# State space layer: u times d moves into the tap matrices, gelu reads PSUM, two direct terms move ahead

## The chip, the cores and the metric

The kernel runs on one core of one Trainium2 chip. The metric is the device time of one execution in microseconds; lower is better. Three runs of the kernel before took 2245.55, 2247.62 and 2248.52 us, median 2247.62. A run of its own was taken with the hardware profiler, and all rows below are from that one.

Engine names: PE (TensorE) multiplies matrices, PEld is its weight load, DVE is VectorE, ACT is ScalarE, POOL is GpSimd, SP is the queue that issues the weight transfers. Each engine runs its own program in order and waits on semaphores for the others.

## The reference, cut to what matters

The program is one block of a first model (state space layer beside a sliding window attention, then a feed-forward layer) and two blocks of a second model. Only the state space layer is touched. `u` is 512 tokens by 512 features, in 32 groups of 16 features with 64 complex states each:

```python
def s5_mixer(u, lam_re, lam_im, log_dt, b_re, b_im, c_re, c_im, d, w_glu, b_glu):
    uf = u.astype(jnp.float32).reshape(bsz, L, SSM_GROUPS, SSM_GROUP)
    ...                                  # discretised a and bbar
    bu_re = jnp.einsum('blgh,gph->blgp', uf, bbar_re)
    bu_im = jnp.einsum('blgh,gph->blgp', uf, bbar_im)
    _, _, xr, xi = lax.associative_scan(_s5_combine, (a_re, a_im, bu_re, bu_im), axis=1)
    y = (jnp.einsum('blgp,ghp->blgh', xr, c_re) - jnp.einsum('blgp,ghp->blgh', xi, c_im)
         + d.astype(jnp.float32) * uf)
    y = jax.nn.gelu(y.reshape(bsz, L, SSM_WIDTH))
    z = y @ w_glu + b_glu
    return z[..., :SSM_WIDTH] * jax.nn.sigmoid(z[..., SSM_WIDTH:])
```

The attention of the same block (8 query heads of 64, window 128) takes q, k and v from the same projection and needs nothing of the state space layer.

## The kernel before, in words

All is kept with features on the 128 partitions and the 512 tokens along the row, so the 512 features of the state space layer are four tiles, i = 0 to 3, of 128x512. PSUM is one tensor `ps` of eight banks of 128x512.

**Time steps in chunks of 4** (`STEP` = 4, 128 chunks). Inside a chunk the output is a convolution: `direct_weights` multiplies out the tap matrices for lags tau = 0 to 3 (128 matmuls of 128x32 into bank 6), ACT copies them to `k_tau`, and `ssm_direct(i)` applies them to `u`: four matmuls of 512, 384, 256 and 128 columns. Between chunks there is a scan: `ssm_in(bt)` takes `u` to the chunk inputs of two tiles (64 matmuls), DVE turns them by cos and sin (`modulate`), scans them along the chunks and turns them back (`demodulate`), and `ssm_out(i)` adds what this gives to the same bank as `ssm_direct(i)` (32 matmuls of 127 columns). Two batches of two tiles: `bt` = 0 holds tiles 0 and 1, `bt` = 1 tiles 2 and 3.

**From there to the GLU.** `ssm_direct` and `ssm_out` of tile i go to bank 6 for even i and to bank 7 (`SUM`) for odd i, so tile 2 can start only when tile 0 has been read (`pre_gelu`). `ssm_chunk(c)` on DVE reads the bank, adds `u` times `d` and writes a row in time order to `tmp`. ACT takes the gelu of it (L1360), then writes the rounded part `x_hi` (`part_hi`), and DVE the rest `x_lo` (`part_lo`). Big products are made of three such parts (`w_lo*x_hi + w_hi*x_lo + w_hi*x_hi`).

**Beside it, the attention.** `turn_tokens1` on PE makes the swapped k and q for the rotary embedding (banks 3 and `Q1_BANKS`) and turns v (bank 0); `rotate1` on DVE finishes each in three passes. Then come 16 steps s. In each PE does `turn1(s)` (turns the weights p), `scores1(s+2)`, `glu_part(s)` (some of the 32 units of the GLU product) and `values1(s-1)`; DVE copies the turned weights (L2136), takes `maximum1(s+2)` and `scale1(s-1)`; ACT takes the exponentials. PE's first scores wait for `kr1_ready`, two of `qr1_ready` and `vt1_ready`; `turn1(0)` waits for the exponentials of step 0; `values1(s)` waits until `scale1(s-1)` has read bank 6 (`o1_ready`).

**What sets the order.** Nothing is scheduled by a planner: each engine's program is written by hand in the order shown. The DVE order around the change is `modulate(0)`, `demodulate(0)`, `modulate(1)`, `demodulate(1)`, `ssm_chunk` 0 and 1, k and q tile 0 rotated, `part_lo` 0 and 1, `ssm_chunk(2)`, q tile 1, `part_lo(2)`, `ssm_chunk(3)`, the two first maxima, `part_lo(3)`, q tile 2, then the 16 steps. The weights come by SP in slabs of up to 1 MB into two slots; the load of slab n is issued when DVE has split slab n-2 (`wlo_ready`).

Of the kernel before, what the change touches and what calls it, by code (L numbers as in the profile page):

```python
# [15 lines left out]
P = 128  # L16
T = 512
# [78 lines left out]
def build(nc, w, x_in, gains_in, lam_in, sink_in, bc_in, c_in, pos_in, iota_in, const_in, freq_in, mask_in, rope2_in,  # L96
# [123 lines left out]
    part_im = at("part_im", where["tmp"] + 4 * KB, [N_PAIR // 2, CHUNKS])  # L220
    pos = at("pos", where["tmp"], [T], i32)
# [26 lines left out]
    def by_phase(bank):  # L248

        return bank.rearrange("p (c l) -> p l c", l=STEP)  # L250

# [104 lines left out]
    v_ready = sem("v_ready")  # L356
    yssm_done = sem("yssm_done")
# [51 lines left out]
    Q1_BANKS = (4, 5, 1, 2)  # L409
    GLU_PER_STEP = [2] * 8 + [3] * 5 + [1, 0, 0]  # L410
# [62 lines left out]
    with nc.Block() as block:  # L473
# [77 lines left out]
        def _(pe):  # L551
# [189 lines left out]
            def direct_weights():  # L741

                for i in range(4):
                    for tau in range(STEP):
                        for ab, cc in ((ab_re, c_re), (ab_neg, c_im)):
                            for q in range(4):
                                at_ = GW * (STEP * i + tau)
                                last = pe.matmul(ps[GW * q:GW * q + GW, 6, at_:at_ + GW], ab[:, tau, 4 * i + q, :],
                                                 cc[:, 4 * i + q, :], start=cc is c_re, stop=cc is c_im)
                last.then_inc(kt_done, 1)  # L750
# [41 lines left out]
            def ssm_direct(i):  # L792
                if i >= 2:
                    pe.wait_ge(pre_gelu, i - 1)
                for tau in range(STEP):
                    pe.matmul(ps[:, (6, SUM)[i % 2], P * tau:T], k_tau[:, i, tau, :],
                              u[:, i, 0:STEP - tau, :].rearrange("p l c -> p (l c)"), start=tau == 0, stop=False,
                              skip_group_check=True)

            def ssm_out(i):  # L800
                for l in range(STEP):
                    for ca, v in ((ca_re, v_re), (ca_im, v_im)):
                        for q in range(4):
                            last = pe.matmul(ps[GW * q:GW * q + GW, (6, SUM)[i % 2], P * l + 1:P * l + P],
                                             ca[:, l, 4 * i + q, :], v[:, 4 * i + q, 0:CHUNKS - 1], start=False,
                                             stop=l == STEP - 1 and ca is ca_im, skip_group_check=True)
                last.then_inc(yssm_done, 1)

            def turn_tokens1():

                pe.wait_ge(bu_free, BATCHES)
                pe.matmul(ps[:, 3, :], swap1, k1[:, :], start=True, stop=True).then_inc(kr1_swap, 1)
                for c in range(4):
                    pe.matmul(ps[:, Q1_BANKS[c], :], swap1, q1[:, c, :], start=True, stop=True).then_inc(qr1_swap, 1)
                for b in range(TB):
                    last = pe.transpose(ps[:, 0, b * P:(b + 1) * P], v1[:, b * P:(b + 1) * P], ident)
                last.then_inc(vt1_done, 1)

# [8 lines left out]
            ssm_in(1)  # L827
            pe.wait_ge(ca_ready, 1)
            for bt in range(BATCHES):
                pe.wait_ge(v_ready, bt + 1)  # L830
                for ii in range(2):
                    if bt:
                        ssm_direct(2 * bt + ii)
                    ssm_out(2 * bt + ii)
                if bt == 0:
                    turn_tokens1()
# [70 lines left out]
            scores1(1)  # L907
            for s in range(16):
# [356 lines left out]
        def _(act):  # L1265
# [88 lines left out]
            act.wait_ge(vt1_done, 1)  # L1354
            act.activation(v1_tok[:, :, :].rearrange("p a c -> p (a c)"), ps[:, 0, :], ACT.Copy).then_inc(vt1_ready, 1)
            for i in range(4):
                act.wait_ge(pre_gelu, i + 1)
                if i >= 2:
                    act.wait_ge(xlo_ready, XB["w_glu"] + i - 1)
                act.activation(tmp[:, 2 + i % 2, :], tmp[:, i % 2, :], ACT.Gelu_apprx_tanh)  # L1360
                act.drain()
                part_hi("w_glu", i, tmp[:, 2 + i % 2, :])
# [353 lines left out]
        def _(dve):  # L1716
# [287 lines left out]
            take(9)  # L2004
            settle()

            def ssm_chunk(c):
                dve.wait_ge(yssm_done, c + 1)
                if c >= 2:
                    dve.wait_ge(xlo_ready, XB["w_glu"] + c - 1)  # L2010
                stt(by_phase(tmp[:, c % 2, :]), u[:, c, :, :], gain("d", c),
                    ps[:, (6, SUM)[c % 2], :].rearrange("p (l c) -> p l c", l=STEP), ALU.mult, ALU.add) \
                    .then_inc(pre_gelu, 1)
# [61 lines left out]
            ssm_chunk(0)  # L2075
            ssm_chunk(1)
# [3 lines left out]
            part_lo("w_glu", 0, tmp[:, 2, :])  # L2080
            part_lo("w_glu", 1, tmp[:, 3, :])
            ssm_chunk(2)
            rotate_q1(1)
            part_lo("w_glu", 2, tmp[:, 2, :])
            ssm_chunk(3)
# [43 lines left out]
            part_lo("w_glu", 3, tmp[:, 3, :])  # L2129
# [637 lines left out]
```

## Time and profile before

| | |
|---|---|
| three runs, median | 2245.55 to 2248.52 us, 2247.62 us |
| the profiled execution, its own time | 2243.69 us |
| its span, first to last instruction | 2241.9 us |
| PE busy | 2137.8 us, 95% |
| DVE busy | 1280.1 us, 57% |
| ACT busy | 886.7 us, 40% |
| chain that ended last, by engine | PE 81%, DVE 11%, DVE's sequencer 4%, ACT 2% |
| mean granted TensorE clock | 0.968 of full |

The profiled execution is 1.79 us longer than its span, and 3.93 us below the median of the three runs. The share of busy time is a mean over the whole program; the stage that is touched is a small piece of it, from about 92 to about 215 us after the start. A row of a timeline says when an instruction (or a merged run of like ones, with its count) started, how long it lasted, and in brackets how long its engine had been idle before it and who ended that. An fp32 matmul stands as two matmul instructions in the trace, so the counts there are twice those of the program.

### The profile page before, as it was taken

The numbers are of one execution on the slowest core, as the hardware profiler recorded it, in microseconds if no ns is written. First come the engines' busy times: TensorE is split into PE (matmuls) and PEld (weight loads), VectorE is DVE, ScalarE is ACT, GpSimd is POOL, SyncE is SP. The second block draws the span as 40 slices with busy tenths as digits, with TensorE's granted clock in tenths as the row PEclk, the third lists the DMA queues.
The fourth block names the chain that finished last, engine by engine and source line by source line (L and its number), as shares of the span: only waits on it lengthen the run. The fifth ranks groups of instructions, "written<-read, shape, count | busy, mean of one in ns | idle before, by whom it ended". The sixth has DMA issues, their size and how long they took to land.

```text
span 2241.9 us, 29415 instructions
## 1 busy us (share of the span) xinstructions
PE 2137.8 (95%) x11002; PEld 1741.6 (78%) x11002; DVE 1280.1 (57%) x2043; ACT 886.7 (40%) x1298; POOL 69.3 (3%) x63
## 2 busy tenths in 40 slices
PE   7969999999999999999988999999999998999997
PEld 5757778888877888888877788888777876888886
DVE  6987454434454666666676642344568886433444
ACT  4225232222227556566552431242345524322322
POOL 1000300000130000000000000000000000000000
PEclk8988999999999999999999899999999998999998
DMA  4102222232232212212221223222112221222221
GB/s 168 30 10 78 93 75 94 86 114 100 71 117 85 85 59 74 85 66 70 80 76 52 76 97 109 94 94 94 57 58 75 75 76 67 102 94 94 94 96 55
DMA packets 31518, 183.46 MB, mean 82 GB/s; under 512 B 5184, under 2 KB 5568, under 8 KB 12736
## 3 DMA queue, kind: packets, MB, share of 16 engines
q1 hardware_dynamic: 27504, 176.18, 23.1%
q10 hardware_dynamic: 3024, 6.00, 0.8%
q8 instruction: 55, 0.90, 0.2%
q0 software_dynamic: 896, 0.06, 0.0%
q14 instruction: 39, 0.32, 0.0%
HBM read 180.06 MB, written 2.10 MB: 81 GB/s over the span
## 4 chain that ended last, share of the span: by engine, by line
PE 81%; DVE 11%; DVEq 4%; ACT 2%; issue 1%; DMA 1%; ACTq 0%
PE ps L569 12%; PE ps L571 12%; PE ps L570 12%; PE ps L1058 6%; PE ps L1060 5%; PE ps L1059 5%; PE ps L1114 2%; PE ps L1115 2%; PE ps L1116 2%; PE ps L630 1%; PE ps L620 1%; PE ps L599 1%; PE ps L625 1%; PE ps L969 1%; DVE f_run L2608 1%
## 5 line engine op out<-in xcount | busy, mean ns | idle before, releaser
L1284 ACT ACTIVATE w_hi<-raw 128x2048 fp32r<-128x2048 f32 (+1 forms) x122 | 226.0, 1853 | 297.1 <-PE ps L571 220.2
L569 PE MATMUL ps<-x_hi,w_lo 128*128 128x512 f32 x816 | 317.6, 389 | 0.5 <-DVE y L2205 0.3
L571 PE MATMUL ps<-x_hi,w_hi 128*128 128x512 f32 x816 | 317.5, 389 | 0.0
L570 PE MATMUL ps<-x_lo,w_hi 128*128 128x512 f32 x816 | 317.4, 389 | 0.0
L1725 DVE TENSOR_TENSOR w_lo<-raw,w_hi 128x2048 fp32r<-128x2048 f32 (+3 forms) x116 | 259.3, 2235 | 93.1 <-ACT w_hi L1284 92.6
L1058 PE MATMUL ps<-x_hi,w_lo 128*128 128x512 f32 x544 | 218.8, 402 | 2.9 <-DVE w_lo L2375 2.4
L1060 PE MATMUL ps<-x_hi,w_hi 128*128 128x512 f32 x544 | 213.1, 392 | 0.0
L1059 PE MATMUL ps<-x_lo,w_hi 128*128 128x512 f32 x544 | 212.5, 391 | 0.0
L569 PEld LDWEIGHTS ps<-x_hi,w_lo 128*128 128x128 f32 x816 | 153.2, 188 | 32.9 <-issue 0.7
L570 PEld LDWEIGHTS ps<-x_lo,w_hi 128*128 128x128 f32 x816 | 153.2, 188 | 31.9
L571 PEld LDWEIGHTS ps<-x_hi,w_hi 128*128 128x128 f32 x816 | 153.2, 188 | 31.8
L571 PE MATMUL ps<-hid_hi,w_hi 128*128 128x512 f32 x378 | 147.1, 389 | 0.0
L569 PE MATMUL ps<-hid_hi,w_lo 128*128 128x512 f32 x378 | 147.0, 389 | 0.0
L570 PE MATMUL ps<-hid_lo,w_hi 128*128 128x512 f32 x378 | 147.0, 389 | 0.0
L2375 DVE TENSOR_TENSOR w_lo<-raw,w_hi 128x2048 fp32r<-128x2048 f32 x38 | 87.0, 2290 | 84.2 <-ACT w_hi L1497 76.6
L2411 DVE TENSOR_TENSOR tmp<-tmp 128x512 f32<-128x512 f32 x64 | 44.3, 692 | 145.6 <-ACT hid_hi L1577 145.5
L1058 PEld LDWEIGHTS ps<-x_hi,w_lo 128*128 128x128 f32 x544 | 102.7, 189 | 24.2 <-DVE w_lo L2375 2.8
L1060 PEld LDWEIGHTS ps<-x_hi,w_hi 128*128 128x128 f32 x544 | 102.5, 188 | 22.4
L1059 PEld LDWEIGHTS ps<-x_lo,w_hi 128*128 128x128 f32 x544 | 102.7, 189 | 19.6
L1539 ACT ACTIVATE swapped<-ps 32x512 f32<-32x512 f32 x192 | 113.2, 590 | 2.3
L1575 ACT ACTIVATE tmp<-ps 128x512 f32<-128x512 f32 x64 | 38.3, 599 | 178.4 <-PE ps L571 175.5
L1530 ACT ACTIVATE qkv<-ps 128x512 f32<-128x512 f32 x72 | 43.0, 598 | 132.0 <-PE ps L1060 131.9
(453 smaller groups left out, 3966.5 us busy)
## 6 DMA issues: line engine op xcount, KB each, us to landing
raw<-w_attn_in SPq DMA_DIRECT2D x32, 1024.0 KB, 5.0
raw<-w_gate_up SPq DMA_DIRECT2D x22, 1024.0 KB, 4.9
raw<-w_up_a SPq DMA_DIRECT2D x16, 1024.0 KB, 4.9
raw<-w_down_a SPq DMA_DIRECT2D x16, 1024.0 KB, 4.9
raw<-w_up_h SPq DMA_DIRECT2D x16, 1024.0 KB, 5.0
raw<-w_down_h SPq DMA_DIRECT2D x16, 1024.0 KB, 4.9
raw<-w_hgrn_in SPq DMA_DIRECT2D x8, 1024.0 KB, 4.9
raw<-w_down SPq DMA_DIRECT2D x8, 768.0 KB, 4.3
```

The costliest lines, as they stand in the source:

```text
L569: pe.matmul(o, w_lo[:, slot, a:a + P], hi[:, k, :], start=k == 0, stop=False)
L570: pe.matmul(o, w_hi[:, slot, a:a + P], lo[:, k, :], start=False, stop=False)
L571: last = pe.matmul(o, w_hi[:, slot, a:a + P], hi[:, k, :], start=False, stop=k == st.kc - 1)
L1058: pe.matmul(o, w_lo[:, slot, a:a + P], x_hi[:, k, :], start=k == 0, stop=False)
L1059: pe.matmul(o, w_hi[:, slot, a:a + P], x_lo[:, k, :], start=False, stop=False)
L1060: last = pe.matmul(o, w_hi[:, slot, a:a + P], x_hi[:, k, :], start=False, stop=k == DC - 1)
L1114: pe.matmul(o, w_lo[:, slot, a:a + P], hi[:, k, :], start=k == 0, stop=False, skip_group_check=True)
L1115: pe.matmul(o, w_hi[:, slot, a:a + P], lo[:, k, :], start=False, stop=False, skip_group_check=True)
L1284: act.activation(w_hi[:, slot, 0:width], raw[:, slot, 0:width], ACT.Copy).then_inc(whi_ready, 1)
L1539: last = act.activation(turned[to:to + 32], bank[at_:at_ + 32], ACT.Copy)
L1725: tt(w_lo[:, slot, 0:width], raw[:, slot, 0:width], w_hi[:, slot, 0:width].bitcast(f32), ALU.subtract) \
L2375: tt(w_lo[:, n0 % 2, :], raw[:, n0 % 2, :], w_hi[:, n0 % 2, :].bitcast(f32), ALU.subtract) \
```

## The change

The term `u*d` is put into the tap matrix of lag 0. DVE makes `d_diag`, the identity times `d` (four 128x128 operations, in the place of the tensor `root`), and `direct_weights` adds it with four matmuls of 128x32 for each of the four tiles. `ssm_chunk` is gone: ACT takes the gelu from the PSUM bank itself and writes it in time order over the tile of `u` that is no longer needed (`glu_in`); `pre_gelu` is now counted by ACT, and `part_hi` and `part_lo` read `glu_in`. A small gelu is issued on ACT ahead of the waits, which puts the table load there. The four tiles have a bank each (`Y_BANKS`), so `ssm_direct(2)` and `ssm_direct(3)` are issued before the first `ssm_out`. The turned v goes to bank 2, and the swaps of q tiles 2 and 3, which share banks with it and with y tile 2, are issued after the two first scores.

The diff, cut to its core:

```diff
@@ -218,6 +218,7 @@
+    d_diag = at("d_diag", where["root"], [4, P])
@@ -248,6 +249,10 @@
+    def glu_in(i):
...
+        return u[:, i, :, :].rearrange("p l c -> p (l c)")
@@ -354,6 +359,7 @@
+    diag_ready = sem("diag_ready")
@@ -407,6 +413,7 @@
+    Y_BANKS = (6, 7, 1, 0)
@@ -740,13 +747,18 @@
+                pe.wait_ge(diag_ready, 1)
...
+                        at_ = GW * (STEP * i + tau)
...
-                                at_ = GW * (STEP * i + tau)
...
-                                                 cc[:, 4 * i + q, :], start=cc is c_re, stop=cc is c_im)
+                                                 cc[:, 4 * i + q, :], start=cc is c_re, stop=cc is c_im and tau > 0)
+                        if tau == 0:
+                            for q in range(4):
+                                last = pe.matmul(ps[GW * q:GW * q + GW, 6, at_:at_ + GW], ident[:, GW * q:GW * q + GW],
+                                                 d_diag[:, i, GW * q:GW * q + GW], start=False, stop=True)
@@ -790,10 +802,8 @@
-                if i >= 2:
-                    pe.wait_ge(pre_gelu, i - 1)
...
-                    pe.matmul(ps[:, (6, SUM)[i % 2], P * tau:T], k_tau[:, i, tau, :],
+                    pe.matmul(ps[:, Y_BANKS[i], P * tau:T], k_tau[:, i, tau, :],
@@ -801,7 +811,7 @@
-                            last = pe.matmul(ps[GW * q:GW * q + GW, (6, SUM)[i % 2], P * l + 1:P * l + P],
+                            last = pe.matmul(ps[GW * q:GW * q + GW, Y_BANKS[i], P * l + 1:P * l + P],
@@ -810,11 +820,14 @@
-                for c in range(4):
-                    pe.matmul(ps[:, Q1_BANKS[c], :], swap1, q1[:, c, :], start=True, stop=True).then_inc(qr1_swap, 1)
+                for c in range(2):
+                    swap_q1(c)
...
-                    last = pe.transpose(ps[:, 0, b * P:(b + 1) * P], v1[:, b * P:(b + 1) * P], ident)
+                    last = pe.transpose(ps[:, 2, b * P:(b + 1) * P], v1[:, b * P:(b + 1) * P], ident)
...
+            def swap_q1(c):
+                pe.matmul(ps[:, Q1_BANKS[c], :], swap1, q1[:, c, :], start=True, stop=True).then_inc(qr1_swap, 1)
@@ -825,12 +838,13 @@
+            pe.wait_ge(tile_free["dve"], STAGES["w_in"].tiles)
+            ssm_direct(2)
+            ssm_direct(3)
...
-                    if bt:
-                        ssm_direct(2 * bt + ii)
@@ -905,6 +919,9 @@
+            pe.wait_ge(pre_gelu, 3)
+            swap_q1(2)
+            swap_q1(3)
@@ -1351,15 +1368,17 @@
-            act.wait_ge(vt1_done, 1)
-            act.activation(v1_tok[:, :, :].rearrange("p a c -> p (a c)"), ps[:, 0, :], ACT.Copy).then_inc(vt1_ready, 1)
+            act.activation(half_glu, gains[:, 0:4], ACT.Gelu_apprx_tanh)
...
-                act.wait_ge(pre_gelu, i + 1)
-                if i >= 2:
-                    act.wait_ge(xlo_ready, XB["w_glu"] + i - 1)
-                act.activation(tmp[:, 2 + i % 2, :], tmp[:, i % 2, :], ACT.Gelu_apprx_tanh)
+                if i == 2:
+                    act.wait_ge(vt1_done, 1)
+                    act.activation(v1_tok[:, :, :].rearrange("p a c -> p (a c)"), ps[:, 2, :], ACT.Copy).then_inc(vt1_ready, 1)
+                act.wait_ge(yssm_done, i + 1)
+                act.activation(glu_in(i).rearrange("p (c l) -> p l c", l=STEP),
+                               ps[:, Y_BANKS[i], :].rearrange("p (l c) -> p l c", l=STEP), ACT.Gelu_apprx_tanh) \
+                   .then_inc(pre_gelu, 1)
...
-                part_hi("w_glu", i, tmp[:, 2 + i % 2, :])
+                part_hi("w_glu", i, glu_in(i))
@@ -2002,15 +2021,11 @@
+            dve.wait_ge(consts_ready, 16)
+            for c in range(4):
+                last = ts(d_diag[:, c, :], ident, gain("d", c), None, ALU.mult)
+            last.then_inc(diag_ready, 1)
...
-            def ssm_chunk(c):
-                dve.wait_ge(yssm_done, c + 1)
-                if c >= 2:
-                    dve.wait_ge(xlo_ready, XB["w_glu"] + c - 1)
-                stt(by_phase(tmp[:, c % 2, :]), u[:, c, :, :], gain("d", c),
-                    ps[:, (6, SUM)[c % 2], :].rearrange("p (l c) -> p l c", l=STEP), ALU.mult, ALU.add) \
-                    .then_inc(pre_gelu, 1)
@@ -2072,17 +2087,12 @@
-            ssm_chunk(0)
-            ssm_chunk(1)
...
-            part_lo("w_glu", 0, tmp[:, 2, :])
-            part_lo("w_glu", 1, tmp[:, 3, :])
-            ssm_chunk(2)
...
-            part_lo("w_glu", 2, tmp[:, 2, :])
-            ssm_chunk(3)
+            for c in range(3):
+                part_lo("w_glu", c, glu_in(c))
@@ -2126,7 +2136,7 @@
-            part_lo("w_glu", 3, tmp[:, 3, :])
+            part_lo("w_glu", 3, glu_in(3))
```

The order on PE, in the middle of the state space layer, before (`ssm_out`'s end, the swaps and turns of k, q and v, the second batch's `ssm_direct` and the first rows of its `ssm_out`):

```order
L804 MATMUL ps<-v_im,ca_im 32x127 x4
L812 MATMUL ps<-k_79,consts 128x512 [waits bu_free]
L814 MATMUL ps<-q_60,consts 128x512 x4
L816 MATMUL ps<-consts,v_80 128x128 x4
L796 MATMUL ps<-u,k_tau 128x512 [waits pre_gelu,v_ready]
L796 MATMUL ps<-u,k_tau 128x384
L796 MATMUL ps<-u,k_tau 128x256
L796 MATMUL ps<-u,k_tau 128x128
L804 MATMUL ps<-v_re,ca_re 32x127 x4
```

And of the changed kernel at the same place:

```order
L814 MATMUL ps<-v_im,ca_im 32x127 x4
L822 MATMUL ps<-k_79,consts 128x512 [waits bu_free]
L830 MATMUL ps<-q_60,consts 128x512 x2
L826 MATMUL ps<-consts,v_80 128x128 x4
L814 MATMUL ps<-v_re,ca_re 32x127 [waits v_ready]
L814 MATMUL ps<-v_re,ca_re 32x127 x3
L814 MATMUL ps<-v_im,ca_im 32x127 x4
```

Between the turned v and `ssm_out` of tile 2 the `ssm_direct` rows and the wait on `pre_gelu` are gone; two of the four q swaps are elsewhere. At the end of that stage, before (from the last `ssm_out` to the first turned weights):

```order
L804 MATMUL ps<-v_im,ca_im 32x127 x4
L850 MATMUL ps<-k_79,q_60 128x128 [waits kr1_ready,qr1_ready,vt1_ready,mask_ready]
L850 MATMUL ps<-k_79,q_60 128x128
L850 MATMUL ps<-k_79,q_60 128x256 x2
L863 MATMUL ps<-consts,p_83 128x128 [waits pre_gelu,p1_ready]
```

And of the changed kernel:

```order
L814 MATMUL ps<-v_im,ca_im 32x127 x4
L864 MATMUL ps<-k_79,q_60 128x128 [waits kr1_ready,qr1_ready,vt1_ready,mask_ready]
L864 MATMUL ps<-k_79,q_60 128x128
L864 MATMUL ps<-k_79,q_60 128x256 x2
L830 MATMUL ps<-q_60,consts 128x512 [waits pre_gelu]
L830 MATMUL ps<-q_60,consts 128x512
L877 MATMUL ps<-consts,p_83 128x128 [waits pre_gelu,p1_ready]
```

The two other q swaps now stand between the first scores and `turn1(0)`. On DVE, from the last pass of `demodulate(1)` to the first maximum, before:

```order
L2055 SCALAR_TENSOR_TENSOR v_im<-v_im,part_im 128x1024
L2011 SCALAR_TENSOR_TENSOR tmp<-u,gains,ps 128x4x128 [waits yssm_done] x2
L2065 TENSOR_TENSOR rot_82<-ps,rope_s 128x512 [waits kr1_swap]
L2066 TENSOR_TENSOR k_79<-k_79,rope_c 128x512
L2068 TENSOR_TENSOR k_79<-k_79,rot_82 128x512
L2065 TENSOR_TENSOR rot_82<-ps,rope_s 128x512 [waits qr1_swap]
L2066 TENSOR_TENSOR q_60<-q_60,rope_c 128x512
L2068 TENSOR_TENSOR q_60<-q_60,rot_82 128x512
L1748 TENSOR_TENSOR x_lo<-tmp,x_hi 128x512 [waits xhi_ready] x2
L2011 SCALAR_TENSOR_TENSOR tmp<-u,gains,ps 128x4x128 [waits xlo_ready,yssm_done]
```

And of the changed kernel:

```order
L2070 SCALAR_TENSOR_TENSOR v_im<-v_im,part_im 128x1024
L2080 TENSOR_TENSOR rot_82<-ps,rope_s 128x512 [waits kr1_swap]
L2081 TENSOR_TENSOR k_79<-k_79,rope_c 128x512
L2083 TENSOR_TENSOR k_79<-k_79,rot_82 128x512
L2080 TENSOR_TENSOR rot_82<-ps,rope_s 128x512 [waits qr1_swap]
L2081 TENSOR_TENSOR q_60<-q_60,rope_c 128x512
L2083 TENSOR_TENSOR q_60<-q_60,rot_82 128x512
L2080 TENSOR_TENSOR rot_82<-ps,rope_s 128x512 [waits qr1_swap]
L2081 TENSOR_TENSOR q_60<-q_60,rope_c 128x512
L2083 TENSOR_TENSOR q_60<-q_60,rot_82 128x512
L1767 TENSOR_TENSOR x_lo<-u,x_hi 128x512 [waits xhi_ready] x3
```

All four `ssm_chunk` rows (L2011) are gone from DVE, and the three first `part_lo` stand together behind the rotations.

## Rows read from the trace of the kernel before

**Rows 1.** Waits of PE from 90 to 215 us: total, times, longest.

```profile
PE ps L796 <- DVE tmp L2011: 10.6, 1, 10.6
PE ps L863 <- ACT stat L1390: 3.5, 1, 3.5
PE ps L804 <- DVEq L2056: 3.0, 1, 3.0
PE ps L796 <- ACT k_tau L1349: 2.5, 1, 2.5
PE ps L748 <- issue: 1.6, 1, 1.6
```

**Rows 2.** Waits of DVE in the same stretch.

```profile
DVE o_tok L2123 <- PE ps L902: 7.3, 10, 1.4
...
DVE tmp L2011 <- PE ps L804: 0.9, 2, 0.6
```

**Rows 3.** Timeline of DVE: start, duration, instruction, count, idle before and who ended it.

```profile
95.89 1.23 DVE L2029 TENSOR_TENSOR v_re<-ps,cos_c 128x1024 f32<-128x1024 f32 x1 [2.27 <-PE ps L788]
...
115.53 1.23 DVE L2029 TENSOR_TENSOR v_re<-ps,cos_c 128x1024 f32<-128x1024 f32 x1 [0.19 <-issue]
...
135.10 2.07 DVE L2011 SCALAR_TENSOR_TENSOR tmp<-u,gains,ps 128x512 f32<-128x512 f32 x2
137.02 0.67 DVE L2065 TENSOR_TENSOR rot<-ps,rope_s 128x512 f32<-128x512 f32 x1
...
140.94 1.29 DVE L1748 TENSOR_TENSOR x_lo<-tmp,x_hi 128x512 fp32r<-128x512 f32 x2
...
147.76 0.34 DVE L2105 CUSTOM_DVE_ANT_0 ps<-ps,masks 128x128 f32<-128x128 f32 x1
...
152.85 0.42 DVE L2136 COPY p_t<-ps 128x256 f32<-128x256 f32 x1
154.40 0.43 DVE L2105 CUSTOM_DVE_ANT_0 ps<-ps,masks 128x256 f32<-128x256 f32 x1 [1.13 <-PE ps L850]
...
158.79 0.43 DVE L2105 CUSTOM_DVE_ANT_0 ps<-ps,masks 128x256 f32<-128x256 f32 x1 [0.37 <-PE ps L850]
...
160.79 0.47 DVE L2123 TENSOR_SCALAR o_tok<-ps,stat 128x64 f32<-128x64 f32 x2 [0.27 <-PE ps L902]
```

**Rows 4.** Timeline of ACT.

```profile
126.43 1.28 ACT L1360 ACT_TABLE_LOAD   x1
136.25 0.63 ACT L1360 ACTIVATE tmp<-tmp 128x512 f32<-128x512 f32 x1 [8.54 <-DVE tmp L2011]
...
149.42 1.28 ACT L1388 ACT_TABLE_LOAD   x1
150.72 0.37 ACT L1388 ACTIVATE p<-ps,stat 128x128 f32<-128x128 f32 x1
```

**Rows 5.** Timeline of PE.

```profile
108.65 3.85 PE L788 MATMUL ps<-u,lw 32*128 32x128 f32 x128
...
121.75 3.60 PE L814 MATMUL ps<-q,consts 128*128 128x512 f32 x8
...
136.36 4.25 PE L796 MATMUL ps<-u,k_tau 128*128 128x512 f32 x8 [10.58 <-DVE tmp L2011]
...
142.42 2.42 PE L796 MATMUL ps<-u,k_tau 128*128 128x512 f32 x8
...
146.64 1.57 PE L850 MATMUL ps<-k,q 64*128 64x128 f32 x8
151.67 0.69 PE L863 MATMUL ps<-consts,p 128*128 128x128 f32 x2 [3.45 <-ACT stat L1390]
...
163.27 1.00 PE L902 MATMUL ps<-v_tok,p_t 128*128 128x64 f32 x8
```

**Rows 6.** Stretches: length, busy PE, PEld, DVE, ACT, POOL, PE clock, DMA share, GB/s.

```profile
151.60:154.00 2.40, 2.33 (x6) 1.45 (x6) 1.59 (x3) 1.96 (x7) 0.00 (x0) 0.50 0.00 0
157.00:160.50 3.50, 3.50 (x19) 2.65 (x18) 2.84 (x12) 0.25 (x1) 0.00 (x0) 0.97 0.00 0
```

## The prediction

> **What bounds the kernel now.** I read the page first, and it says little here: PE is busy 95% of the span, but as a mean over the whole program. The stage that is touched lies between 92 and 215 us, and there the waits of PE come first [rows 1]. These five are all that PE waits for in that stretch. The longest, 10.6 us, is before `ssm_direct(2)`: PE waits for DVE's `ssm_chunk(0)`. The next, 3.5 us, is before `turn1(0)`: PE waits for ACT's first exponentials. After 151.67 us PE waits for nothing until 215. So the stage has two halves: up to about 152 us DVE's program is the path, with no idle time from 115.53 on but the short waits for PE; after that PE is. The timeline of DVE shows the first half [rows 3]: `demodulate(1)` has just ended when two `ssm_chunk` start at 135.10, then come rotations, `part_lo`, two more `ssm_chunk`, and the first maximum at 147.76. The timelines of ACT and PE show what hangs on that: the first exponential at 150.72 [rows 4] and `turn1(0)` at 151.67 after 3.45 us of idle time [rows 5]. PE pays twice: in the stretch after that idle time it is granted 0.50 of its clock (1.2 GHz), and it is back at 0.97 only in the stretch from 157.0 [rows 6].
>
> **Edits that I cost at nothing.** *d_diag on DVE*: four operations of 128x128. Nearest are 0.34 (first maximum, 128x128) and 0.67 (128x512) [rows 3], so 1.4 to 2.7 us; I take 1.4, by size. They stand where DVE waited 2.27 us for `ssm_in(0)` [rows 3]; at the upper bound all would be 0.4 us later. *16 more matmuls in direct_weights*: `ssm_in` has 64 matmuls in 3.85 us [rows 5], 0.06 each, so at most 1.0 us, and not below 0. They push `ssm_in(1)`, whose end was 112.50; DVE asks for it at 115.53 [rows 3]. Cover 3.0 us. *ssm_direct(2) and (3) early*: 2.42 us each at full clock [rows 5], so PE goes on from about 113 to 118, and where it waited 3.0 us [rows 1] the first `ssm_out` is some 2 us later. That result goes to ACT now, and nobody needs tiles 0 and 1 before about 141. Then come the k swap, two q swaps (four took 3.60, so 0.9 each [rows 5]) and the turned v. Before, all this ended 10.58 us ahead of 136.36; that idle time is the cover, and PE still waits in it for DVE. *The table load ahead*: it changes nothing, for the load was early already: it ran at 126.43 while its gelu had to wait until 136.25 [rows 4].
>
> **DVE's path, step by step.** From 135.10, where the first `ssm_chunk` stood:
> - three rotations (k, q tiles 0 and 1): two took 140.94 - 137.02 = 3.92, so 1.96 each, 5.9: 141.0.
> - three `part_lo` at 1.29 for two, about 0.6 each: 142.8. All need ACT's `x_hi`; for tile 2 see below.
> - the first maximum at 142.8 and not 147.76: 5.0 us earlier. That is what four `ssm_chunk` cost (two in 2.07, so some 4.1) and the 0.9 that they waited for PE [rows 2].
> - from there to the copy of step 0, 152.85 - 147.76 = 5.1: 147.9.
> - the next maximum came 1.55 later, 1.13 of it waiting for PE. PE will have done those scores, so 148.3.
> - to the maximum after that 158.79 - 154.40 = 4.4, less 0.37 idle: 152.3.
> - to the scaling L2123 2.0, less 0.27 idle, and 0.47 for itself: 154.5. This lets `values1(1)` go.
>
> **PE and ACT beside it.** PE starts `ssm_out(2)` at 135.2. One tile takes 146.64 - 142.42 - 2.42 = 1.8 at full clock. After idle time of this length `ssm_direct(2)` took 4.25 against 2.42 for its twin, so at the lower clock. Two tiles take 3.6 at the higher and 7.2 at the lower; starting low and rising as late as in that row (136.36 + 4.25, so 4.2 us in, with 2.1 us of the work done), 140.9. Gelu of tile 2 is done by 140, of tile 3 by 141.5 (0.63 each), its `x_hi` by 142.2, the exponential's table (1.28) by 143.8 at the latest. The first scores start when q tile 1 is rotated, 141.0, against 146.64. The two q swaps behind them add 1.8, so PE is ready for `turn1(0)` at about 144.4. The first exponential needs the first maximum and its small operations, 1.2 us: 144.1. `turn1(0)` followed 0.95 later: 145.0, not 151.67. From `turn1(0)` to `values1(1)` PE took 163.27 - 151.67 = 11.6 us. Of these, 5.3 (up to 157.0) ran at half clock; PE will have idled less than 1 us this time and not 3.45, so I count them at full clock, 2.7: 8.9 us in all, so 153.9. DVE's 154.5 is later, and the `values1(1)` of before at 163.27 becomes 154.6: **8.7 us** earlier.
>
> **The sum.** From 163.27 on PE waited for nothing up to 215 [rows 1], and DVE waited 7.3 us for PE's values in ten places [rows 2], so DVE catches up and the 8.7 us stay. Every transfer is asked for when DVE has split a slab, and moves with it. The profiled execution took 2243.69, so 2243.69 - 8.7 = 2235.0; the median of the three runs is 3.93 above it, so **2239 us** is the forecast. Of the 8.7, 5.0 are DVE's work and waits gone, 1.8 its waits for PE in the first steps (1.13 + 0.37 + 0.27), and the other 1.9 that PE came to `values1(1)` that much after DVE had let it go, since it had been slow.
>
> **Two rules weighed.** The rows of the tables first: the exponential ran right at the end of its table load: 149.42 + 1.28, then 150.72 [rows 4]. The Trainium skill, page "ScalarE: Activation LUTs", section "What ACT_TABLE_LOAD costs", counts a drain of 1380 ns on top, 2.66 us in all. By the page the first exponential would come at about 145.1, and the sum would be 8.5; the trace bears that out in no row. Second: `ssm_chunk`, which wrote its row in steps of four elements, took 1.04 each where an ordinary pass took 0.67 [rows 3]. The Trainium skill, page "SBUF — State Buffer", its note on "cachelines", says that an access that goes to a new 16-byte line pays a penalty; the gelu now writes in just such steps. If it grows by the same 0.4 us, tile 3's comes at 141.9 and the table at 144.2: the sum stays.
>
> **The rivals.**
> - *TensorE comes cold to the steps again.* For: it idles some 10 us before 135.2, as before, and the clock may rise later than I take it. If `ssm_out` runs wholly at the lower clock, it ends at 142.4, the scores and swaps at twice their time (3.1 + 3.6) at about 149, and `values1(1)` at 149 + 8.9 = 158: 5.3 us gained. If it rises in time and falls again for `turn1(0)`, 145.0 + 11.6 = 156.6 leaves 6.7; both at once about 2.6. Middle 5: 2242.6. Against: in the trace it had risen by the end of the 4.25 us row.
> - *DVE's pace is all there is.* The steps follow DVE, and only its 5.0 us arrive: 2242.6. Against: its 7.3 us of waiting in the loop.
> - *Taken back.* Short matmuls in an unbroken row ran out of instructions once: 1.6 us within `direct_weights`, for which the profile shows no cause but issue [rows 1]. Now 16 more stand there and `ssm_out(2)`, `(3)` and the scores have no break. Two or more such stops on the path, with something late after the loop, leave under 4.5 us: about 2245.
> - *Slower: TensorE stays at the lower clock through the steps.* PE would now meet DVE in each step with short waits where before it was full. The stretch from 151.67 to 157.0 shows the price: 2.7 us lost in 5.3. If all of the 60 us of steps ran so, 30 us would be lost: 2239 + 30 = 2269. It takes over the gain from 17 us of steps at the lower clock. Against: the waits I find are under 1 us, and the steps of before held 0.97 once they had begun to fill [rows 6].
>
> **Chances.** Forecast 0.70 (its own range 2236 to 2241.5, three runs differing by 3 us); cold start 0.13; DVE's pace 0.08; taken back 0.05; slower 0.04. Two parts in a thousand, 4.5 us, are about what a measurement of this kernel can tell from no change. Faster by more: all of the forecast, two thirds of the next two, 0.84. Within it 0.12. Slower 0.04. Range 2235.5 to 2244: below, a warmer loop than I count; above, the mixed forms of the first three rivals.
>
> **What will show it.** No wait of PE for DVE's `tmp`; PE's idle time before `ssm_out(2)` about 10 us, ending near 135.2; the first maximum near 142.8; the first exponential near 144.1; PE idle under 1 us before `turn1(0)`, with the full clock there; `values1(1)` near 154.6 with a short wait for L2123's successor; from there the same steps as before. I am wrong if the clock from 141 to 150 is low, if gelu from PSUM takes well over 1 us, or if the distance at 163 us is 8.7 and is less at 215.

## The result, and the profile after

| | before | after |
|---|---|---|
| median of 4 runs each | 2246.85 us | 2233.03 us (2230.09 to 2234.72) |
| ratio, 95% interval | | 0.9944 (0.9928 to 0.9961) |
| the profiled execution, its span | 2243.69, 2241.9 us | 2233.89, 2232.1 us |
| mean granted TensorE clock | 0.968 | 0.972 |

The change gains 13.8 us where 8.7 were forecast; 2233.03 lies 2.5 us below the range. The direction was right, the size was not. The fourth run of the kernel before brought its median down by 0.8 us, from 2247.62 to 2246.85; that part of the distance to 2239 is not the change's.

PE's waits from 90 to 215 us of the changed kernel (line waited for, us in total, times, longest), against [rows 1]:

```profile
PE ps L814 <- DVEq L2071: 8.3, 1, 8.3
PE ps L756 <- issue: 4.0, 2, 2.5
PE ps L806 <- ACT k_tau L1366: 2.6, 1, 2.6
PE ps L877 <- ACT stat L1409: 0.9, 1, 0.9
```

The wait for `tmp` (10.6) is gone, as is the one ahead of the first `ssm_out` (3.0): the direct terms of tiles 2 and 3 are done there now. What is left is the one ahead of `ssm_out(2)`, and before `turn1(0)` (L877) 0.9 stands where 3.5 stood. Within `direct_weights` (L756) PE now stood still twice, 4.0 us and not 1.6, with no cause but issue.

DVE's timeline (start, us, instruction, idle time before it and who ended it), against [rows 3]:

```profile
97.54 1.22 DVE L2044 TENSOR_TENSOR v_re<-ps,cos_c 128x1024 f32<-128x1024 f32 x1 [1.48 <-PE ps L800]
...
117.95 1.22 DVE L2044 TENSOR_TENSOR v_re<-ps,cos_c 128x1024 f32<-128x1024 f32 x1 [0.97 <-PE ps L800]
...
137.51 0.69 DVE L2080 TENSOR_TENSOR rot<-ps,rope_s 128x512 f32<-128x512 f32 x1
...
145.22 0.29 DVE L2115 CUSTOM_DVE_ANT_0 ps<-ps,masks 128x128 f32<-128x128 f32 x1
...
156.19 0.48 DVE L2133 TENSOR_SCALAR o_tok<-ps,stat 128x64 f32<-128x64 f32 x2
```

The four `ssm_chunk` are gone. But `modulate(1)` now waits 0.97 us for `ssm_in(1)`, so it comes 20.41 us after `modulate(0)` and not 19.64 [rows 3]. From it the first maximum is 27.27 us away, where it was 32.23.

ACT's timeline, against [rows 4]:

```profile
106.91 1.28 ACT L1371 ACT_TABLE_LOAD   x1
...
124.26 1.18 ACT L1377 ACTIVATE u<-ps 128x512 f32<-128x512 f32 x1 [15.85 <-PE ps L814]
...
143.77 1.12 ACT L1377 ACTIVATE u<-ps 128x512 f32<-128x512 f32 x1 [0.78 <-PE ps L814]
...
145.75 1.28 ACT L1407 ACT_TABLE_LOAD   x1
147.04 0.37 ACT L1407 ACTIVATE p<-ps,stat 128x128 f32<-128x128 f32 x1
```

The gelu's table is loaded 17 us ahead of its use. The gelu that writes in time order takes 1.12 us, not 0.63 [rows 4], so the exponential's table comes 0.5 us later than forecast, and the exponential again starts right behind its load.

PE's timeline, against [rows 5]:

```profile
103.99 0.24 PE L756 MATMUL ps<-c_im,ab_neg 128*32 128x32 f32 x5 [2.45 <-issue]
...
106.95 7.08 PE L806 MATMUL ps<-u,k_tau 128*128 128x512 f32 x16 [2.56 <-ACT k_tau L1366]
113.95 3.85 PE L800 MATMUL ps<-u,lw 32*128 32x128 f32 x128
...
137.47 0.65 PE L814 MATMUL ps<-v_re,ca_re 128*32 128x127 f32 x8 [8.34 <-DVEq L2071]
...
143.65 1.55 PE L864 MATMUL ps<-k,q 64*128 64x128 f32 x8
145.13 1.99 PE L830 MATMUL ps<-q,consts 128*128 128x512 f32 x4
147.99 0.44 PE L877 MATMUL ps<-consts,p 128*128 128x128 f32 x2 [0.88 <-ACT stat L1409]
...
149.42 0.50 PE L895 MATMUL ps<-x_hi,w_lo 128*128 128x512 f32 x1
...
157.06 1.00 PE L916 MATMUL ps<-v_tok,p_t 128*128 128x64 f32 x8
```

`ssm_out(2)` starts at the lower clock (0.65 a group, 0.40 a group from 142.9 on), but from `turn1(0)` on nothing is slow: `values1(1)` comes 9.07 us behind it, not 11.6 [rows 5]. In the windows 148.0 to 150.3 and 150.3 to 157.0 the granted clock is 1.00, where it was 0.50 [rows 6].

**Where the rest came from.** The stage explains about half. The other half lies 500 to 1000 us later, in code that the change does not touch. Three windows of the kernel before (window, its length, busy time and instructions of PE, PEld, DVE, ACT and POOL, then PE's granted clock, DMA share, GB/s):

```profile
700.00:725.00 25.00, 22.62 (x107) 17.95 (x106) 11.67 (x21) 15.80 (x27) 0.00 (x0) 0.93 0.25 85
1180.00:1215.00 35.00, 30.58 (x154) 23.73 (x151) 20.67 (x49) 8.04 (x16) 0.00 (x0) 0.90 0.17 53
1232.00:1250.00 18.00, 14.79 (x54) 11.85 (x54) 10.39 (x18) 5.64 (x6) 0.00 (x0) 0.53 0.17 58
```

The same pieces of the program in the changed kernel:

```profile
700.00:725.00 25.00, 22.62 (x127) 17.89 (x125) 14.02 (x23) 16.37 (x26) 0.00 (x0) 1.00 0.25 85
1173.00:1208.00 35.00, 30.45 (x167) 23.91 (x167) 22.95 (x53) 9.19 (x18) 0.00 (x0) 1.00 0.19 57
1224.00:1242.00 18.00, 13.71 (x49) 10.27 (x50) 12.63 (x20) 5.64 (x6) 0.00 (x0) 0.62 0.17 59
```

The granted clock is the third figure from the end: 0.93, 0.90 and 0.53 against 1.00, 1.00 and 0.62. What PE did ahead of the second place is the same in both, a wait of 2.2 us for ACT. The turned weights behind that wait, before:

```profile
1187.39 1.43 PE L969 MATMUL ps<-consts,p 128*128 128x128 f32 x8 [2.17 <-ACT p L1512]
```

And after:

```profile
1180.95 1.09 PE L986 MATMUL ps<-consts,p 128*128 128x128 f32 x8 [2.15 <-ACT p L1531]
```

The eight turns take 1.43 us in one and 1.09 in the other after the same idle time. The table sums this up for all kernels by the distance between the same matmuls of PE's program, in the one trace of each, us (times in the first column are those of before):

| stretch | before, twice | after, twice | taps alone | early alone | before +1.7 | before +2.9 |
|---|---|---|---|---|---|---|
| 92 to 156 | 63.2, 63.0 | 56.0, 56.1 | 63.0 | 61.3 | 63.5 | 63.0 |
| 156 to 199 | 43.4, 43.4 | 42.8, 42.7 | 44.2 | 42.8 | 43.6 | 43.3 |
| 199 to 226 | 26.6, 26.6 | 27.8, 27.7 | 26.8 | 26.8 | 26.7 | 26.6 |
| 226 to 317 | 90.8, 90.8 | 91.1, 91.2 | 91.0 | 90.8 | 90.8 | 90.8 |
| four places: 711 to 780, 1167 to 1272 in three parts | 174.6, 174.6 | 168.7, 168.6 | 168.7 | 175.0 | 169.1 | 168.6 |

So in the stage 7.8 us are gained (7.2 + 0.6), 1.5 are given back up to 317 us, and 5.9 come from the four places. That makes 12.2; the two profiled executions show only 9.8 since the one of after came 1.6 us late to 92 us, by waits at the program's start that its second trace doesn't have, and lost 0.8 in small pieces elsewhere. The 13.8 us of the medians are 1.6 more than the 12.2. Both traces of before are of quick executions (2243.69 and 2243.54, medians 2246 to 2247), so the rest can't be located in them.

What is given back at the end of the steps is the clock again, the other way round. The stretch at the lower level lasts 13.6 us in the kernel before and 17.1 us in the changed one; first before, then after:

```profile
211.80:225.40 13.60, 10.53 (x40) 8.95 (x39) 8.94 (x25) 6.15 (x13) 0.00 (x0) 0.50 0.59 199
204.20:221.30 17.10, 14.17 (x55) 12.47 (x56) 11.31 (x30) 7.89 (x17) 0.00 (x0) 0.50 0.51 181
```

### The profile page after: what moved, and what is told of

It reads as the page before. It is cut to its first block, busy times and chain, and to the rows that moved or that the text cites. A ratio compares the mean times of both kernels' runs of the same rounds, so it can differ in the third digit from the quotient of the medians.

```text
span 2232.1 us, 29475 instructions
## 1 busy us (share of the span) xinstructions
PE 2130.8 (95%) x11034; PEld 1737.3 (78%) x11034; DVE 1276.1 (57%) x2043; ACT 888.2 (40%) x1299; POOL 69.3 (3%) x63
## 4 chain that ended last, share of the span: by engine, by line
PE 83%; DVE 9%; DVEq 4%; ACT 2%; issue 2%; DMA 1%; ACTq 0%
PE ps L577 12%; PE ps L576 12%; PE ps L578 12%; PE ps L1075 6%; PE ps L1077 5%; PE ps L1076 5%; PE ps L1131 2%; PE ps L1133 2%; PE ps L1132 2%; DVE f_run L2618 1%; PE ps L637 1%; PE ps L627 1%; PE ps L697 1%; PE ps L606 1%; PE ps L607 1%
```

## The experiments

The theory after the result (B): besides the stage's gain, the change shifts what follows, and later places of low clock fall away, whatever made the shift. The rival (A): the gain above 8.7 is in the stage, or chance of four runs.

**Both kernels again**, unedited.

> The changed kernel once more. Theory A (chance): the stage itself gives what its trace shows, 6.2 us from 97 to 163 us plus 1.6 us that this execution had lost earlier, 7.9 in all; the rest of the measured 13 us is the phase of TensorE's clock, other in each execution. Then five more runs give a ratio to the kernel before between 0.9955 and 0.9970 (7 to 10 us). Theory B (systematic): something in the change saves 4 to 5 us more in every execution. Then the ratio is 0.9935 to 0.9950 again (11 to 15 us).

> The kernel before once more, for its spread and a second trace. Both theories: ratio 1.000. Theory A: the slow stretches of TensorE's clock lie elsewhere than in its first trace, and the stretches 0-95, 215-750 and 1160-1260 us move by 1 to 3 us each against the first trace though the program is the same. Theory B: the two traces of before agree within 1 us at every place outside the stage, and the median of before is high since the stage itself (90 to 215 us) is slower than in its first trace by 3 us or more.

After: 2230.4 (5 runs), ratio 0.9932 (0.9912 to 0.9952). Before: 2245.98 (11 runs), 0.9998 (0.9987 to 1.0009). Both new traces repeat their columns of the table to 0.3 us. Not chance, and not in the stage: A falls. One half of B fell with it: the stage of before is no slower in the second trace (63.0 against 63.2), so it doesn't explain why its median lies above both traces. The mean granted clock of the runs without a trace points to the same cause as the places: among 31 runs of the kernel before that were taken beside the padded kernels below, the three quickest (2239.1 to 2240.4) had 0.972 to 0.973 and the four slowest (2249.3 to 2249.9) 0.967 to 0.968; the five of after had 0.973 to 0.976.

**Each half alone.** Taps alone keeps the two banks and the late `ssm_direct`:

```diff
-    Y_BANKS = (6, 7, 1, 0)
+    Y_BANKS = (6, 7, 6, 7)
+                if i >= 2:
+                    pe.wait_ge(pre_gelu, i - 1)
-            ssm_direct(2)
-            ssm_direct(3)
+                    if bt:
+                        ssm_direct(2 * bt + ii)
```

> The changed kernel with one part undone: tiles 2 and 3 use banks 6 and 7 again and their direct terms come after ssm_out(1), as before; u*d in the taps, gelu from PSUM and the early table stay. If DVE's work is what counts, 5 us (ratio 0.9978) of gain stay. If, as I hold, both parts are needed because PE is next in line, the direct terms (4.25 + 2.42 us) come back between 135 and 146 us, the first scores start near 146, and only 2 to 3 us stay (ratio 0.9987 to 0.9993).

Early alone keeps `ssm_chunk` and `u*d` on DVE in the kernel before, with the four banks:

```diff
-                    pe.matmul(ps[:, (6, SUM)[i % 2], P * tau:T], k_tau[:, i, tau, :],
+                    pe.matmul(ps[:, Y_BANKS[i], P * tau:T], k_tau[:, i, tau, :],
+            ssm_direct(2)
+            ssm_direct(3)
```

> The kernel before with the other part alone: four banks, direct terms of tiles 2 and 3 early, two swaps later; DVE's ssm_chunk stays. If PE's late direct terms were the bound, 4 us or more are gained (ratio 0.998). If DVE's path is the bound, only its waits of 0.9 us for PE go and the table of the exponential stays behind the last gelu: 1 to 2 us (ratio 0.9992 to 0.9997).

Taps alone: 2240.2, ratio 0.998 (0.9968 to 0.9993). Early alone: 2242.43, 0.9982 (0.9971 to 0.9992). PE's timeline of taps alone:

```profile
136.91 4.63 PE L808 MATMUL ps<-u,k_tau 128*128 128x512 f32 x8 [9.85 <-DVEq L2069]
...
147.88 1.57 PE L865 MATMUL ps<-k,q 64*128 64x128 f32 x8
152.21 0.55 PE L878 MATMUL ps<-consts,p 128*128 128x128 f32 x2 [2.75 <-ACT stat L1407]
```

DVE is free 5 us sooner, and it helps nobody: PE does `ssm_direct(2)` slowly (4.63) after 9.85 us of idle time, and the scores start at 147.88, after which PE waits 2.75. The stage gains nothing (63.0 and 44.2, 0.6 more than before), and yet the kernel is 4.5 us faster by the ratio: its four places take 168.7. PE's two long waits of early alone, and what follows the second:

```profile
PE ps L803 <- DVEq L2062: 10.7, 1, 10.7
PE ps L853 <- DVE q L2074: 5.2, 1, 5.2
```

```profile
145.77 2.90 PE L853 MATMUL ps<-k,q 64*128 64x128 f32 x8 [5.17 <-DVE q L2074]
148.60 3.73 PE L819 MATMUL ps<-q,consts 128*128 128x512 f32 x4
```

Here PE is early and waits 5.2 us for DVE's rotated q, which `ssm_chunk` delays; scores and swaps then run at half speed (2.90 and 3.73). The stage gains 2.5, the places nothing (175.0). The halves gain -0.6 and 2.5, together 7.8: each removed one of two chains that end within a few us of each other. The ratios would have misled: 0.998 for taps alone is what was expected if DVE's work were what counts, and 0.9982 for early alone what was expected if PE's direct terms were the bound. Only the distances within the stage show that neither half does it.

**Work added ahead of the places**, which should only cost. One, two or four matmuls ahead of `gate_up1`, a product of the feed-forward layer, at about 486 us; the two were:

```diff
+                    for cols in [512, 512]:
+                        pe.matmul(ps[:, 6, 0:cols], ident, rope_c[:, 0:cols], start=True, stop=True)
```

> The kernel before with two extra fp32 matmuls of 512 columns (1.7 us at full clock, result unused) on PE ahead of gate_up1, at about 400 us, where PE is the path. Plain theory: every stage after it is as long as before and the kernel is 1.7 us slower (2247.2 to 2247.7). Phase theory: the granted clock falls at fixed places of the program only if the chip's own rhythm meets them so, and the 5.5 us between 215 and 1250 us that the changed kernel saved without any change there are such places; then the segments 649-713, 1167-1195 and 1233-1249 us change length by 1 to 2.5 us each and the sum is not 1.7.

> As the last, with 1740 columns (2.9 us). Plain theory: 2.9 us slower than before, about 2248.6. Phase theory: this puts the program where the changed kernel was against the rhythm of the clock, the three segments take the lengths of the changed kernel (1.2, 2.3 and 1.2 us less) and the kernel is 1 to 3 us faster than before although it does more work: 2243 to 2245.

> The changed kernel with one extra matmul of 300 columns (0.5 us) at the same place. Plain theory: 0.5 us slower than the changed kernel, 2231.5 to 2232. Phase theory: it moves to where the kernel before was, loses the 4.7 to 5.5 us again, and takes 2236 to 2238.

> The changed kernel with 1.7 us of extra matmuls there. Plain theory: 1.7 us slower than the changed kernel, about 2233. Phase theory: the three segments change by 1 to 2.5 us each in either direction; any total but 1.7 more, between 2229 and 2239.

Before with 1.7 us more: 2242.42, ratio 0.9986 (0.9977 to 0.9996), so faster with more work; its places take 169.1. (Its first place did run at the lower clock, but from its first matmul on, ahead of where the table starts to count; counted from that matmul, its places take 171.0 where before took 175.5.) Before with 2.9 us more: 2243.96, 0.9996 (0.9985 to 1.0007), places 168.6, 6.0 less against 2.9 more; the runs show 0.9 of the 3.1, which is no clear difference. These two traces show B: work added far from the places takes 4.5 to 6 us out of them. After with 0.5 us more: 2237.81 (2231.29 to 2239.73), 0.9964 (0.9953 to 0.9976); after with 1.7: 2235.24, 0.9964. The first lost 5 to 7 us for 0.5. That fits B, but where it was lost isn't shown: its one trace is of its quickest run, with the places at 168.6. The padded kernels also show that the pattern isn't fixed by the program: the runs of after with 1.7 us more fall in two groups, 2233.5 to 2235.2 (6) and 2238.4 to 2241.1 (5).

**The input product first.** In the changed kernel, `ssm_in(1)` right behind `direct_weights`, ahead of `ssm_direct(0)`:

```diff
+            ssm_in(1)
             ssm_direct(0)
             ssm_direct(1)
-            ssm_in(1)
```

> The changed kernel with ssm_in(1) issued before the wait for k_tau, right behind direct_weights. In the changed kernel DVE waited 0.97 us for ssm_in(1), since direct_weights stood still twice (4.0 us, issue) and everything of PE behind it was late. Theory: the 0.97 us wait goes, and the distance from modulate(0) to values1(1), 59.5 us in the changed kernel, becomes 58.4 to 58.7. Rival: PE's lateness does not matter there and it stays 59.5. The total is expected anywhere between 2226 and 2236, since the later segments change with the clock's rhythm; the distance decides.

2231.18 (6 runs), ratio 0.9944 (0.9928 to 0.9961). DVE's two `modulate`:

```profile
95.28 1.23 DVE L2044 TENSOR_TENSOR v_re<-ps,cos_c 128x1024 f32<-128x1024 f32 x1 [1.49 <-PE ps L800]
...
114.92 1.22 DVE L2044 TENSOR_TENSOR v_re<-ps,cos_c 128x1024 f32<-128x1024 f32 x1 [0.19 <-issue]
```

The wait is gone and the distance is 19.64 us again, though the stops within `direct_weights` stayed at 4.0. The distance that was to decide came out between the two: `values1(1)` stands at

```profile
154.31 1.00 PE L916 MATMUL ps<-v_tok,p_t 128*128 128x64 f32 x8
```

so 59.0 us behind `modulate(0)`, where 59.5 was after and 58.4 to 58.7 the expectation. Of the 0.8 us won at `modulate(1)` 0.5 arrived; the stage took 55.5. The median can't tell it from after.

**PE kept at work.** On top of the last edit, ten matmuls in PE's idle time ahead of `ssm_out(2)`, and the same with the products by `rope_c` on POOL:

```diff
+                pe.wait_ge(pre_gelu, 2)
+                for _ in range(10):
+                    pe.matmul(ps[:, 7, :], ident, rope_c[:, :], start=True, stop=True)
```

```diff
+            pool.tensor_tensor(k1[:, :], k1[:, :], rope_c[:, :], ALU.mult).then_inc(rope_half, 1)
-                tt(tile, tile, rope_c[:, :], ALU.mult)
+                dve.wait_ge(rope_half, nth)
```

> e9 with ten extra matmuls of 512 columns on PE (8.5 us, result unused) in the idle time ahead of the second ssm_out. Theory (cold start): ssm_out(2) and (3) took 6.2 us since the granted clock was 0.5; warm they take 3.7, the last gelu, its x_hi and the exponential's table come 2.4 us earlier, and the distance from modulate(0) to values1(1) shrinks by 0.5 to 2 us against e9 (57 to 58), as DVE is then the path. Rival: the lower clock there costs nothing because DVE is the path anyway; the distance stays as in e9.

> e10 with the products by rope_c of k and the four q tiles taken from DVE and given to POOL, which is idle then (1.04 us each in the first trace against 0.6 on DVE). If DVE is the path once PE is warm, three products less ahead of the first maximum and two more later are 2 to 3 us: distance 54.5 to 56. If POOL and DVE slow each other, or PE and ACT are the path, under 1 us.

With the matmuls, 2230.11 (6 runs), ratio 0.9945. PE's timeline:

```profile
127.81 5.31 PE L830 MATMUL ps<-rope_c,consts 128*128 128x512 f32 x12
135.22 0.42 PE L814 MATMUL ps<-v_re,ca_re 128*32 128x127 f32 x8 [2.10 <-DVEq L2074]
...
141.40 2.80 PE L867 MATMUL ps<-k,q 64*128 64x128 f32 x8 [2.50 <-DVE q L2086]
144.12 3.78 PE L833 MATMUL ps<-q,consts 128*128 128x512 f32 x4
147.69 0.63 PE L880 MATMUL ps<-consts,p 128*128 128x128 f32 x2
...
157.02 1.00 PE L919 MATMUL ps<-v_tok,p_t 128*128 128x64 f32 x8
```

`ssm_out(2)` and `(3)` now take 3.7 us instead of 6.2, and nothing is won: the first maximum comes 27.28 us after `modulate(1)`, as in after (27.27), since DVE's rotations set it. The lower clock has moved to the scores and swaps (2.80 and 3.78), and there it costs: `turn1(0)` starts 32.0 us behind `modulate(1)` and not 30.0, and the distance from `modulate(0)` to `values1(1)` is 61.0 us, 1.9 longer than in the last kernel, where 57 to 58 or no change had been expected. The median doesn't show it. Its six runs are the plainest sign of two patterns: 2229.5 to 2230.6 (4), and 2237.2 and 2238.4. The profiled one is the last, and its window at the second place reads as that of before:

```profile
1174.00:1209.00 35.00, 30.59 (x155) 23.80 (x155) 20.67 (x50) 8.03 (x16) 0.00 (x0) 0.90 0.16 53
```

On POOL: 2236.53 (10 runs), ratio 0.9969. POOL's products, and DVE's scans beside them:

```profile
121.36 1.27 POOL L531 TENSOR_TENSOR k<-k,rope_c 128x512 f32<-128x512 f32 x1 [70.99 <-PE ps L829]
122.59 2.73 POOL L534 TENSOR_TENSOR q<-q,rope_c 128x512 f32<-128x512 f32 x2
```

```profile
121.40 1.51 DVE L2065 TENSOR_TENSOR_SCAN s_re<-par,v_re 128x128 f32<-128x128 f32 x1
...
124.18 1.42 DVE L2065 TENSOR_TENSOR_SCAN s_re<-par,v_re 128x128 f32<-128x128 f32 x1
125.52 0.39 DVE L2065 TENSOR_TENSOR_SCAN s_im<-par,v_im 128x128 f32<-128x128 f32 x1
```

A scan takes 1.4 to 1.5 us while POOL runs and 0.39 behind it; three of them cost 3.2 us. The first maximum is 28.87 us after `modulate(1)`, 1.6 later, and `values1(1)` 61.2 us behind `modulate(0)` (155.78 - 94.62), where 54.5 to 56 had been hoped for. A miss.

**The gelu's write.** It writes in the order in which it reads, so tokens are permuted in the output; the small gelu ahead is left out too.

```diff
-            act.activation(half_glu, gains[:, 0:4], ACT.Gelu_apprx_tanh)
-                act.activation(glu_in(i).rearrange("p (c l) -> p l c", l=STEP),
-                               ps[:, Y_BANKS[i], :].rearrange("p (l c) -> p l c", l=STEP), ACT.Gelu_apprx_tanh) \
+                act.activation(glu_in(i), ps[:, Y_BANKS[i], :], ACT.Gelu_apprx_tanh) \
```

> The changed kernel without the small gelu on ACT ahead of the waits, and with gelu writing its row in the order in which it reads it, so that the tokens of the state space layer come out permuted. Step on the table: the load still runs right behind the k_tau copies, some 15 us ahead of its gelu, so nothing is late. Step on the write: if steps of four elements are what makes gelu take 1.12 us, it takes 0.63 here; if reading from PSUM is the reason, it stays near 1.1.

One run, 2230.2 us. ACT's timeline:

```profile
139.41 0.60 ACT L1376 ACTIVATE u<-ps 128x512 f32<-128x512 f32 x1 [11.39 <-PE ps L814]
...
143.17 1.28 ACT L1405 ACT_TABLE_LOAD   x1
144.66 0.37 ACT L1405 ACTIVATE p<-ps,stat 128x128 f32<-128x128 f32 x1 [0.20 <-DVE stat L2119]
```

0.60 us instead of 1.12: the price of the gelu is the stepped write, not PSUM. The exponential now waits for DVE and not for its table, and PE waited 0.25 before `turn1(0)`. The stage took 54.8, 1.2 less than after, but little of that is the gelu's: `modulate(1)` waited 0.39 and not 0.97, and `values1(1)` came 38.9 us behind it against 39.1.

## Why the prediction was wrong

**The failed step is in "The sum"**: "so DVE catches up and the 8.7 us stay", with every transfer moving along. I took all that follows 163 us as one rigid block, so its 2080 us had no term and no uncertainty. There the same work took 5.9 us less (four places, at the higher clock where before it was at the lower), and 1.5 more up to 317 us. My range allowed below 2236 only "a warmer loop" in the stage. Traces of kernels without any gain in the stage (taps alone), or with work added to the kernel before, show 4.5 to 6 us of it too.

**The stage itself** came as worked out. From the start of `modulate(1)`, forecast and measured (after):

| | forecast | after |
|---|---|---|
| first maximum | 27.3 | 27.27 |
| first exponential | 28.6 | 29.09 |
| `turn1(0)` | 29.5 | 30.04 |
| `values1(1)` | 39.1 | 39.11 |

- *DVE's path* (5.0): right to 0.1 us.
- *ACT*: the stepped gelu took 0.5 more than I set in the sum. I had named this and called it harmless; it was 0.5 us late for the exponential and `turn1(0)`.
- *`values1(1)`* (39.1): right by some luck. I had DVE let it go, 0.6 us behind PE, with a short wait of PE. No such wait is there: DVE had finished its scaling at 38.7, and PE, 0.5 late at `turn1(0)` and 0.2 slower in the loop, came last at 39.1. With the plain gelu `turn1(0)` came 0.6 us earlier (29.4), PE did wait for DVE (0.2), and `values1(1)` came only 0.2 earlier.
- *PE's clock*: it rose 5.1 us into `ssm_out`, and not 4.2; both tiles took 6.2 us and not 5.7, and the first scores came 25.7 us behind `modulate(1)` against 25.5 forecast. The loop at full clock (9.07 against 8.9) was right. The first rival (cold again, 2242.6) didn't come in the changed kernel; a part of it did with ten matmuls added, where scores and swaps at the lower clock cost 1.9 us.
- *16 matmuls for at most 1.0 us, cover 3.0 us*: wrong. The stops for issue grew from 1.6 to 4.0 us, `ssm_in(1)` was late by 0.97, and the stage gained 7.8 instead of 8.7. Putting `ssm_in(1)` first took the wait away and brought 0.5 back. Why there are more stops isn't settled; taps alone has them (4.4) and early alone hasn't (1.3), so they come with the taps, by the 16 matmuls most likely; no run adds those alone.
- *Table load ahead*: nothing, as forecast; without it the first gelu waited for PE just the same.
- *"If the distance at 163 us is 8.7 and is less at 215"*: this sign of being wrong came in part. The gain was 7.9 us at `values1(1)` and 6.4 at 226 us, when the longer stretch at the lower clock had passed.
- *Two slips in the working*, neither in the sum: with the exponential at 145.1 the steps given lead to 154.95, so 8.3 us and not 8.5; and steps that take 60 us at the full clock would lose near 60 us at half of it, not 30.

**What stays open**: what decides which pattern a place takes. The time at which it is reached doesn't sort the traces: the first place (its first matmul behind the wait) ran at the full clock when reached at 702.5, 704.4, 710.6 and 712.2 us, and fell when reached at 703.2, 707.2, 709.2 and 713.3. Nor do the places go together: with POOL the first ran at the full clock and the second at the lower. The Trainium skill, page "TensorE: Matmul & The Clock Gate", section "What's actually happening", says that the count of slow matmuls varies between runs of one kernel, and that the penalty is under 1% of a typical span. On the size the traces agree: 6 us are 0.27%. That the count varies within one kernel no two traces here show at these places; the two groups of run times are a sign of it. And 6 us are two thirds of the gain that was forecast here.

## What to carry to other kernels

When a program waits a few us in many places, add a term for the clock of the untouched rest to every forecast: list the places where the granted clock is low, take them once at either level, and put that on both sides of the sum. Here it would have been at least 6 us below. To judge an edit, compare the same matmuls' distance within the stage; the total may change for a reason that a padding of two matmuls brings too. And look for the second chain before pricing the removal of the first: the halves of this change gained -0.6 and 2.5 us, both together 7.8.

## What the hardware showed unexpectedly

- After the same idle time of 2.2 us ahead of the same matmuls, the granted clock over the 35 us around it was 1.00 in one kernel's execution and 0.90 in another's (33.9 us against 36.6 from matmul to matmul).
- POOL's two-input products beside DVE's scans: 1.4 to 1.5 us a scan against 0.39, about one POOL instruction (1.3 us) each. The Trainium skill, page "SBUF — State Buffer", section "SBUF: two separate sides", says that a DVE operation with two SBUF inputs and a GpSimd operation that reads SBUF hold a shared port pair exclusively, the other waiting for the whole instruction; the trace agrees.
- An ACT pass over 128x512 that writes with a step of four elements took 1.12 us, and 0.60 in plain order, both from PSUM.
- PE ran out of instructions twice (1.6 and 2.5 us) in a run of 288 very short matmul instructions, and once (1.6) in one of 256.
